# Modulation columns straight from 32-wide weight blocks, and feature norms as rows on column groups

## The reference, cut to what matters

```
mod   = silu(c) @ w_mod + b_mod            # 6*1024 columns, for c and for c_ctx: two vectors
h     = rmsnorm(x) * (1 + sc1) + sh1       # parts 0 and 1 of mod
p     = h @ w_in                           # 42 chunks of 128 columns (one of them narrower)
q     = rmsnorm(p_q) @ w_uq ; ckv = rmsnorm(p_kv)
o_hg  = rmsnorm(o_f + o_b) * silu(hg)      # four heads, gated linear recurrence
...                                        # attention, merge, ConvGLU, final norm
```

## Time and profile before

| | us |
|---|---|
| median of 3 runs | 2057.23 |
| lowest and highest | 2057.1, 2061.9 |
| the profiled execution | 2058.16 |
| its span | 2056.4 |
| TensorE busy | 1994.0 |
| TensorE weight loads busy | 1837.9 |
| VectorE busy | 1120.0 |
| ScalarE busy | 766.7 |
| GpSimd busy | 831.9 |

### The profile page before, as it was taken

How to read it: one execution, slowest core, us unless ns; L and a number is a source line. 1 busy time by engine, 2 the same in 40 slices (tenths; PEclk the granted TensorE clock), 3 DMA queues, 4 the chain that set the end, 5 groups by cost and what they waited for, 6 DMA issues and landing times.

```text
span 2056.4 us, 34056 instructions
## 1 busy us (share of the span) xinstructions
PE 1994.0 (97%) x13708; PEld 1837.9 (89%) x13708; DVE 1120.0 (54%) x1715; ACT 766.7 (37%) x1189; POOL 831.9 (40%) x595
## 2 busy tenths in 40 slices
PE   6999999999999989999999988999999999999998
PEld 5888999999999978887799877999999999988886
DVE  5314353526142047566535356988888888645363
ACT  4323233333223254767733234322222222353441
POOL 1225263535133235455535634433443443252441
PEclk9999999999999999999999999999999999999999
DMA  8563111112213284324266445422222231584661
GB/s 294 200 199 37 42 51 44 48 52 74 67 41 90 72 227 143 93 67 107 73 173 202 147 149 189 125 77 65 86 65 65 75 98 59 175 304 141 230 237 67
DMA packets 223310, 244.09 MB, mean 119 GB/s; under 512 B 57865, under 2 KB 184162, under 8 KB 223154
## 3 DMA queue, kind: packets, MB, share of 16 engines
q1 hardware_dynamic: 220962, 233.65, 37.3%
q0 software_dynamic: 2192, 8.26, 1.2%
HBM read 182.62 MB, written 59.26 MB: 118 GB/s over the span
## 4 chain that ended last, share of the span: by engine, by line
PE 53%; DVE 3%; DMA 3%; ACT 2%; POOL 1%; issue 1%; SPq 1%; DVEq 0%; ACTq 0%; POOLq 0%
PE late_psum L2938 22%; PE late_psum L2950 13%; PE late_psum L1876 4%; PE late_psum L1901 4%; PE late_psum L2897 3%; PE late_psum L2251 3%; PE late_psum L1511 1%; PE late_psum L1846 1%; DMA s_w_raw<-in_w_hg_o 1%; DVE p_lo L2056 1%; DMA scratch_extra<-e_lo 1%; DMA merge_gates<-scratch_gates 0%; DVE conv L3124 0%; ACT prob L1987 0%; PE late_psum L1515 0%
## 5 line engine op out<-in xcount | busy, mean ns | idle before, releaser
L688 PE MATMUL s_psum<-h_hi,s_w_hi 128*128 128x384 f32 x984 | 333.3, 344 | 6.4 <-DVE h_lo L1402 6.4
L688 PE MATMUL s_psum<-h_hi,s_w_lo 128*128 128x384 f32 x984 | 326.1, 337 | 0.0
L688 PE MATMUL s_psum<-h_lo,s_w_hi 128*128 128x384 f32 x984 | 325.9, 337 | 0.0
L131 POOL TENSOR_TENSOR s_w_lo<-s_w_raw,s_w_hi 128x1024 fp32r<-128x1024 f32 x41 | 100.0, 2440 | 337.0 <-ACT s_w_hi L126 337.0
L2938 PE MATMUL late_psum<-h_lo,ffn_w_hi 128*128 128x320 f32 (+1 forms) x704 | 208.5, 296 | 0.0
L2938 PE MATMUL late_psum<-h_hi,ffn_w_lo 128*128 128x320 f32 (+1 forms) x704 | 208.4, 296 | 0.0
L2938 PE MATMUL late_psum<-h_hi,ffn_w_hi 128*128 128x320 f32 (+1 forms) x704 | 208.3, 296 | 0.0
L688 PEld LDWEIGHTS s_psum<-h_hi,s_w_hi 128*128 128x128 f32 x984 | 185.5, 189 | 15.8 <-issue 14.0
L688 PEld LDWEIGHTS s_psum<-h_lo,s_w_hi 128*128 128x128 f32 x984 | 186.1, 190 | 0.0
L688 PEld LDWEIGHTS s_psum<-h_hi,s_w_lo 128*128 128x128 f32 x984 | 185.8, 189 | 0.0
L2873 POOL TENSOR_TENSOR u_lo<-u_raw,u_hi 128x384 fp32r<-128x384 f32 x66 | 112.9, 1719 | 162.5 <-ACT u_hi L2770 161.5
(11 more groups left out here) (371 smaller groups left out, 4709.9 us busy)
## 6 DMA issues: line engine op xcount, KB each, us to landing
w_raw<-in_w_ffn_out SPq DMA_DIRECT2D x66, 512.0 KB, 3.7
ffn_raw<-in_w_ffn_in SPq DMA_DIRECT2D x44, 512.0 KB, 5.3
s_w_raw<-in_w_in SPq DMA_DIRECT2D x41, 512.0 KB, 4.3
s_w_mod<-in_w_mod SPq DMA_DIRECT2D x8, 2048.0 KB, 8.3
scratch_u<-conv SPq DMA_DIRECT2D x22, 576.0 KB, 3.6
u_raw<-scratch_u SPq DMA_DIRECT2D x66, 192.0 KB, 5.2
scratch_gates<-sig SPq DMA_DIRECT2D x48, 192.0 KB, 1.9
merge_gates<-scratch_gates SPq DMA_DIRECT2D x16, 576.0 KB, 4.8
```

The lines of the kernel that those rows point to most:

```text
L131: pool.tensor_tensor(flat[0], flat[1], flat[2], ALU.subtract).then_inc(self.lo_ready, 1)
L688: return pe.matmul(slot_bank(s), weights(c)[wx][:, k, :], hx[:, k, j * CH:(j + 1) * CH], start=(k == 0 and n == 0), stop=(k == KD - 1 and ...
```

## The change

The stationary operand and the moving one change places in the modulation product: for each of the 8 k-steps and each 128 columns of w_mod, four blocks of 32 weight columns are made stationary, on the four column groups, and the two columns of `cc` move; the result is a column at once, summed over k in PSUM. `cc` has two columns instead of 32. The copies to `m_rows` and `mod_rows`, `sel` and the row-to-column matmuls go. Because the pieces now alternate between banks 7 and 6, VectorE clears 384 columns of both at the start. In the six norms the ones are stationary, 32 wide, and 384 squares move, once for each third of the tokens, each third on its own column group; root and reciprocal run over 96 partitions x 384; the broadcast has one row of ones stationary and one row of 384 reciprocals moving, on three row groups. `R`, `kv_rb`, `q_rb` and what follows q_rb come one slot later, the first two levels of `K` of head 0 one slot sooner. At the start ScalarE splits the first two weight chunks ahead of its last take of x.

```diff
+ROWS = slice(0, NCH * BLOCK)
     def pe_sums(self, pe, psum):
         pe.wait_ge(self.acc_ready, self.kts - 1)
-        for t in range(TILES):
-            last = pe.matmul(psum[:, t:t + 1], self.acc[:, t * P:(t + 1) * P], self.cst.ones[:, 0:1], start=True, stop=True)
+        for g in range(NCH):
+            last = pe.matmul(psum[BLOCK * g:BLOCK * (g + 1), 0:CH], self.cst.ones[:, 0:BLOCK], self.acc[:, g * CH:(g + 1) * CH],
+                             start=True, stop=True)
...
-        dve.reciprocal(self.stat[:, TILES:2 * TILES], self.stat[:, 0:TILES]).then_inc(self.rstd_ready, 1)
+        dve.reciprocal(self.stat[ROWS, :], self.stat[ROWS, :]).then_inc(self.rstd_ready, 1)
...
-        for t in range(TILES):
-            last = pe.matmul(psum3[:, t // 3, (t % 3) * P:(t % 3 + 1) * P],
-                             self.stat[:, TILES + t:TILES + t + 1].to_broadcast([P, P]), self.cst.ident[:, :],
-                             start=True, stop=True)
+        for g in range(NCH):
+            row = slice(BLOCK * g, BLOCK * g + 1)
+            last = pe.matmul(psum3[:, g, 0:CH], self.cst.ones[row, :], self.stat[row, :], start=True, stop=True)
...
-            at[a + lv - 1].append(("K", h, lv))
+            at[a + lv - 1 - (h == 0 and lv <= 2)].append(("K", h, lv))
-        for r, kind in ((9, "X"), (10, "U"), (12, "O"), (13, "S"), (14, "R")):
+        for r, kind in ((9, "X"), (10, "U"), (12, "O"), (13, "S"), (15, "R")):
...
+                def columns_of(weights_m, at, to_bank, to):
+                    for k in range(KD):
+                        for a in range(0, P, BLOCK):
+                            cc_last[0] = pe.matmul(psum[a:a + BLOCK, to_bank, to:to + 2], weights_m[:, k, at + a:at + a + BLOCK],
+                                                   cc[:, k, :], start=(k == 0), stop=(k == KD - 1))
                 def piece_product(i):
                     pe.wait_ge(p_loaded[i], 32)
...
-                    else:
-                        pe.wait_ge(p_rows, i)
-                    for part in range(2):
-                        for quad in range(4):
-                            k = 4 * part + quad
-                            last = pe.matmul(psum[32 * quad:32 * quad + 32, 6, :], cc[:, k, :], pieces[i][:, k, :],
-                                             start=(part == 0), stop=(part == 1))
+                    if i >= 2:
+                        pe.wait_ge(p_mod, i - 1)
                     for x in range(2):
                         for j in range(QK):
+                            columns_of(pieces[i], x * QW + j * P, 7 - i % 2, 4 * x + 2 * j)
+                    cc_last[0].then_inc(p_ps, 1)
...
-                        if c == 0 and k + 1 < QUARTERS:
-                            piece_columns(k + 1)
...
                 def mod_product(n):
                     pe.wait_ge(wm_loaded[n % 2], 16 * (n // 2 + 1))
                     if n == 0:
                         freed(pe, 2 * NCH - 1)
                     for j in range(4):
+                        columns_of(w_mod[n % 2], j * P, 5, 8 * n + 2 * j)
+                    cc_last[0].then_inc(mod_ps, 1)
...
-                x_take(2 * TILES - 1)
-                take_piece(0)
                 split(0)
                 split(1)
+                x_take(2 * TILES - 1)
...
+                dve.memset(psum[:, 6:8, 0:CH], 0.0).then_inc(banks_clear, 1)
```

More of the change, by code:

```diff
@@ L454, in stage_project @@
         pieces = piece_a + [first(f"w_mod_b{i}", [P, KD, 2 * QW]) for i in range(2)]
-        m_rows = [first(f"m_rows{i}", [P, 2, QW]) for i in range(2)]
         first_end = first.at
-        last = Arena(nc, low.sig_at - 2 * NT * 4 - KD * 32 * 4)
-        cc = last("cc", [P, KD, 32])
+        last = Arena(nc, low.sig_at - 2 * NT * 4 - KD * 2 * 4)
+        cc = last("cc", [P, KD, 2])
         y = [last(f"a1_y{i}", [P, NT]) for i in range(2)]
@@ L475, in stage_project @@
         near = early("hg_near", [P, TILES, SIDE])
[L476 to L478 removed]
+        orow = early("ostat", [P, CH])
         lbt = early("lbt", [P, 24])
[L480 removed]
+        assert early.at <= low.sig_at - 2 * NT * 4 - KD * 2 * 4
         over = Arena(nc, early_end)
@@ L759, in mod_product @@
                     pe.wait_ge(wm_loaded[n % 2], 16 * (n // 2 + 1))
-                    if n >= 2:
-                        pe.wait_ge(mod_row, n - 1)
-                    for i in range(2):
-                        for quad in range(4):
-                            k = 4 * i + quad
-                            last = pe.matmul(psum[32 * quad:32 * quad + 32, 6 + n % 2, :], cc[:, k, :], w_mod[n % 2][:, k, :],
-                                             start=(i == 0), stop=(i == 1))
-                    last.then_inc(mod_ps, 1)
-                def mod_columns(n):
-                    pe.wait_ge(mod_row, n + 1)
                     if n == 0:
@@ L773, in mod_columns @@
                     for j in range(4):
-                        a = 8 * n + 2 * j
-                        last = pe.matmul(psum[:, 5, a:a + 2], mod_rows[n % 2][:, j * P:(j + 1) * P], sel[:, 0:2],
-                                         start=True, stop=True)
-                    last.then_inc(modt_ps, 1)
+                        columns_of(w_mod[n % 2], j * P, 5, 8 * n + 2 * j)
+                    cc_last[0].then_inc(mod_ps, 1)
                 def item(kind, h, lv):
@@ L881, in item @@
                         pe.wait_ge(osq_ready, 3 * h + 3)
-                        for t in range(TILES):
-                            last = pe.matmul(psum[:, S_BANK, t:t + 1], osq[:, t * P:(t + 1) * P], cst.ones[:, 0:1],
-                                             start=True, stop=True)
+                        for g in range(NCH):
+                            last = pe.matmul(psum[BLOCK * g:BLOCK * (g + 1), S_BANK, 0:CH], cst.ones[:, 0:BLOCK],
+                                             osq[:, g * CH:(g + 1) * CH], start=True, stop=True)
                         last.then_inc(s_ps, 1)
@@ L888, in item @@
                         pe.wait_ge(gated_ready, 3 * h + 3)
-                        for t in range(TILES):
-                            last = pe.matmul(psum[:, rb_bank(t // 3), (t % 3) * P:(t % 3 + 1) * P],
-                                             ostat[:, TILES + t:TILES + t + 1].to_broadcast([P, P]), cst.ident[:, :],
-                                             start=True, stop=True)
+                        for g in range(NCH):
+                            row = slice(BLOCK * g, BLOCK * g + 1)
+                            last = pe.matmul(psum[:, rb_bank(g), 0:CH], cst.ones[row, :], orow[row, :], start=True, stop=True)
                         last.then_inc(rb_ps, 1)
```

76 lines of the change are left out of this document (22 added, 54 removed).

## The result

The changed kernel takes 2093.9 us in the median of four runs (2092.1 to 2094.4), the kernel before 2057.2 beside it: ratio 1.0177 [1.0152 to 1.0203], 36.7 us slower. The forecast was 2072 us, so the direction was right and less than half of the size was forecast; 2093.9 lies at the upper edge of the range, 2 us from the 2092 of rival C.

A forecast was written before the change was run, and what follows sets the result against it. TensorE was taken as the bound, busy 1994.0 of 2056.4 us. Terms +0.7 + 20 + 8 - 11.4 - 0.5 - 2 = +14.8 on 2058.2 gave 2073.0, the median 0.9 lower: 2072 us, range 2043 to 2094.

The forecast's parts named there:

- rival C: Slab slots: TensorE idles some 3 us in each of eight and falls to 1.2 GHz; +15, 2092 in all; chance 0.14.
- TensorE's own time of the columns: Modulation products, twelve slabs: 33.6 us of TensorE time after against 32.9 before, +0.7 us (-4 to +10).
- Late instruction blocks: Slots 6 to 13: instruction fetches wait for slab loads in flight, +2.5 us a slot, +20 us over eight.
- The start: Before the first w_in product: late blocks in the early modulation pieces put it at 48.2 us; +8 (-5 to +14).
- Pieces 2 and 3: Last two early modulation pieces, after the first w_in product: they meet no load and cost +3.1 us together.
- The norms: Six norms: sums 1.2 us and broadcasts 0.7 us shorter each, -11.4 us in all (-6 to -14).
- open question of the row groups: Norm broadcasts: three one-row matmuls take 0.75 us side by side or 2.1 one behind the other; 1.2 taken.
- Slot 18: Slot with the four stores: most of its 9.45 us loss was expected to come again; -2 (-9 to +5).
- Rival B: Whole kernel: instruction blocks arrive in time or nearly so, under 1 us lost a burst; 2042 us; chance 0.28.

The follow-up runs named there:

- 64-wide blocks: The changed kernel with 64-wide instead of 32-wide stationary blocks in the modulation column products: 2075.3 us, ratio 1.0072.
- bursts with 32 columns: The changed kernel with 32 moving columns (30 of them zeros) in place of 2 in each modulation product: 2090.7 us, ratio 1.0159.
- spread kernel: The changed kernel with each slab's column products in four groups of 64 inside the slot's bank product, instead of one burst of 256: 2107.9 us, ratio 1.0234.

## Why the forecast was too small, step by step

- **TensorE's own time of the columns** (+0.7): right at full clock. 9.7 ns a record against the 11.0 taken; a fed slot has 6.95 us against 7.02.
- **Late instruction blocks** ("Modulation columns, instructions", +20, 2.5 us a slot): the term that failed. The eight slots and what stands with them lost 31.3 us (forecast 20.7 less 0.5). What was expected was there (idle "issue" inside the bursts, 130 packets, five in the first 50 us), and the idle time alone, 18.4 us more, is near the 20. But that nearness is luck: the 2.5 us came from a block that waits for the slab load in flight, and removing the loads gave 4.7 us of the 31.3. In its place the runs show a turn of some 3.5 us for every block, which a burst that enters two blocks 1.25 us apart cannot cover. The price also had nothing in it for the clock.
- **The clock** (rival C, at 0.14, at nothing in the sum): TensorE was busy 13.0 us longer at the lower level, and this is what the price of 2.5 us a slot lacked. Rival C had +15 for it and 2092 in all, and 2092 is what was measured, within 2 us. I had held against it that idle times of 3 us are too short, and here they were 3.65 us at most. Its own reason, the idle time, is not shown either: with 64-wide blocks the clock was 0.85 with no idle time at all. Idle time and clock are not two prices that simply add: in bursts with 32 columns 4.5 us less busy time came with 3.7 us more idle time. Only in the spread kernel, at 0.57, was the clock the limit alone.
- **The start** (+8): the first product came at 48.75, forecast 48.2, for the reason given: three blocks came late in the first two pieces, one of them 6.7 us after the one before it, behind dense loads. Pieces 2 and 3 were forecast at +3.1 and cost 6.5 (95.27 - 48.75 = 46.5 against 82.87 - 42.85 = 40.0), 4.2 us of idle time and the rest busy time at a lower clock. VectorE's gain took 0.16 us instead of 2.00, as forecast (the reason given for it was not tried), and the first product came later all the same.
- **The norms** (-11.4): right, and the open question of the row groups is settled: three one-row products run side by side, 0.86 us against the 1.2 taken and the 2.1 estimated for one behind the other. Alone they are worth 13.5 us.
- **Slot 18** (-2, bounds -9 to +5): 14.34 against 14.65; slot 17 lost 1.1 us. The stores were named as the cause and are, in both kernels.

Of the 19.1 us between 14.8 and 33.9, the slabs are 11.1, the start 4.4, and what follows 3.6 (-9.75 against -13.4).

Rival B (2042) fell. The Trainium skill, page "Runtime: NRT & Kernel Launch", section "Instruction fetch mechanics", says that dispatch is slower than the fill, which is why the fetch is hidden. Here TensorE took 134 records with their loads in 1.30 us, some 206 instructions a microsecond, and had the next 256 some 3.5 us after entering the ones before, 74 a microsecond; the trace disagrees for streams of short matmuls. The pauses 128 records apart at the start agree with the page's blocks of 256.

What stays open: why a packet starts 1.1 us after the block before it is entered and TensorE goes on only 1.2 us after it has landed; why dense loads delay some packets by up to 3 us and others not; and which property of the products the granted clock answers to. For the last, the runs show only that 32 moving columns raised it and that it was low with 64-wide blocks without idle time. No run changed the size or the order of the packets.

## What to carry to other kernels

Count the instructions of a stretch beside its engine time, and ask how soon one block of 256 follows another. Here a block needed about 3.5 us from the moment the one before was entered, so splitting a product into small blocks costs time as soon as 256 matmuls and weight loads go through faster than that, even if the average looks harmless. In each of eight slots 48 instructions turned into 512, and that cost 31 us in all although the work at full clock did not change. When the engine idles with "issue" as its reason, look at what else is in flight: moving four small stores gave 9.7 us. And test the parts of a change apart, since here one was worth -13.5 us and the other +49.

## What was not expected of the hardware

- Four stores of single 4-byte elements stretched one instruction packet from about 1.1 to 5.3 us, and the slot lasted 9.5 us longer, 4.7 of them idle. Dense loads did not stretch a packet (1.1 us), but some packets started up to 3 us later behind them.
- A block of 256 TensorE instructions was ready 3.5 us after the block before it was entered, though its own transfer took 1.1 us.
- 128 records of 64-wide blocks with 2 moving columns took 3.90 us, of 32-wide blocks 1.25 us: 30.5 against 9.8 ns.
- In the spread kernel the granted clock stayed at 0.50 for over 80 us with TensorE busy all the time, after one idle time of 3.6 us; with 32 moving columns in the same order it was 0.94 over the stretch.
